# A fused two-block transformer kernel on one core: the gated unit in rounded halves, and the second head's first weights queued earlier

## What is computed

```python
# first block, per head h of 8 (weights of 128 columns each)
q, k, v, lx, ly = h_in @ w_in[...]              # five products 256x2048 by 2048x128
xc = causal_conv(lx); r, i = sigmoid(xc @ w_a), sigmoid(xc @ w_x)
a = exp(-8 r softplus(-lam)); state = scan(a, sqrt(1 - a*a) * i * xc)
attention(q, k, v); state * gelu(ly)
# second block, after the state-space scan
y = gelu(ssm(u)); y = y * sigmoid(y @ w_glu + b_glu)   # the gated unit, w_glu 2048x2048
out = (y * silu(z)) @ w_out
```

## Time and profile before

| | us |
|---|---|
| median of three runs (lowest, highest) | 3626.04 (3616.76, 3626.87) |
| profiled execution | 3616.24 |
| its span | 3614.5 |
| TensorE busy | 3435.4 (95% of the span) |
| VectorE busy | 2457.7 (68%) |
| ScalarE busy | 1337.0 (37%) |

### The profile page before, as it was taken

How to read it: one execution, slowest core, us unless ns; L and a number is a source line. 1 busy time by engine, 2 the same in 40 slices (tenths; PEclk the granted TensorE clock), 3 DMA queues, 4 the chain that set the end, 5 groups by cost and what they waited for, 6 DMA issues and landing times. The chain is left out here.

```text
span 3614.5 us, 56289 instructions
## 1 busy us (share of the span) xinstructions
PE 3435.4 (95%) x20628; PEld 3038.4 (84%) x20628; DVE 2457.7 (68%) x4574; ACT 1337.0 (37%) x1960; POOL 354.0 (10%) x400
## 2 busy tenths in 40 slices
PE   3899999999999999999999998999999899999998
PEld 2688887889777999999999997676679898999998
DVE  7666556867487777777777777888835634666665
ACT  1232311013244444444444444211112434555553
POOL 0010110000000000000000000677710000000000
PEclk8999999999999999999999999999999999999999
DMA  9678743446777888888888885222247644555543
GB/s 404 269 302 302 273 168 128 157 144 235 288 286 292 294 295 294 291 292 296 296 295 296 296 293 200 82 89 91 91 171 253 253 144 138 187 187 184 184 171 139
DMA packets 123316, 817.71 MB, mean 226 GB/s; under 512 B 12848, under 2 KB 18224, under 8 KB 27184
## 3 DMA queue, kind: packets, MB, share of 16 engines
q1 hardware_dynamic: 105696, 761.31, 58.4%
q10 hardware_dynamic: 17488, 54.58, 4.0%
HBM read 791.65 MB, written 24.18 MB: 226 GB/s over the span
## 5 line engine op out<-in xcount | busy, mean ns | idle before, releaser
L526 PE MATMUL bank<-H,ring 128*128 128x256 f32 x3680 | 828.8, 384 | 30.3 <-PEq L371 13.4
L526 PEld LDWEIGHTS bank<-H,ring 128*128 128x128 f32 x3680 | 696.9, 192 | 149.8 <-issue 51.3
L1833 DVE TENSOR_TENSOR vlo<-ring,vhi 128x1024 fp32r<-128x1024 f32 x448 | 547.4, 1225 | 289.1 <-ACT vhi L1241 287.8
L1241 ACT ACTIVATE vhi<-ring 128x1024 fp32r<-128x1024 f32 x448 | 474.0, 1060 | 606.9 <-PE bank L596 315.0
L562 PE MATMUL bank<-Hhi,whi 128*128 128x256 f32 x1920 | 484.9, 290 | 20.9 <-DVE Hlo L1530 9.6
L1519 DVE TENSOR_TENSOR wlo<-ring,whi 128x1024 fp32r<-128x1024 f32 x240 | 293.9, 1232 | 304.7 <-ACT whi L1054 301.4
L563 PE MATMUL bank<-Hlo,whi 128*128 128x256 f32 x1920 | 475.1, 285 | 0.0
L589 PE MATMUL bank<-vhi,Ghi 128*128 128x512 f32 x1024 | 402.0, 393 | 15.2 <-ACT vhi L1241 15.2
L590 PE MATMUL bank<-vhi,Glo 128*128 128x512 f32 x1024 | 401.1, 392 | 0.0
L562 PEld LDWEIGHTS bank<-Hhi,whi 128*128 128x128 f32 x1920 | 370.8, 193 | 31.0 <-issue 17.7
L541 PE MATMUL bank<-Fhi,vhi 128*128 128x256 f32 x1536 | 373.0, 279 | 1.1 <-ACT vhi L1241 1.1
(11 more groups left out here) (422 smaller groups left out, 4374.2 us busy)
## 6 DMA issues: line engine op xcount, KB each, us to landing
ring<-in_peer_u SPq DMA_DIRECT2D x128, 1024.0 KB, 5.7
ring<-in_peer_v SPq DMA_DIRECT2D x128, 1024.0 KB, 5.9
arena<-in_w_mod SPq DMA_DIRECT2D x96, 1024.0 KB, 7.1
ring<-in_w_ada SPq DMA_DIRECT2D x72, 1024.0 KB, 7.1
ring<-in_w_qz SPq DMA_DIRECT2D x64, 1024.0 KB, 4.8
ring<-in_w_in SPq DMA_DIRECT2D x35, 1024.0 KB, 7.3
ring<-in_ssm_in SPq DMA_DIRECT2D x32, 1024.0 KB, 5.0
ring<-in_w_mod SPq DMA_DIRECT2D x32, 1024.0 KB, 5.0
```

Source lines behind the costliest of these rows:

```text
L526: last = mm(out, ring[:, pos % R, k, :], rhs[:, k, :], start=(k == 0), stop=(k == KT - 1))
L1241: A(vhi[:, half], v_half(pos, half), ACT.Copy).then_inc(s("vhi_ready"), 1)
L1833: v.tensor_tensor(vlo[:, half], v_half(pos, half), vhi[:, half].bitcast(F32), ALU.subtract)\
```

## The change

Three edits:

1. The gated unit's 16 products go from `gemm` to `gemm_split`. ScalarE and VectorE now also make high and low parts of Y after the gelu (`Yhi`, `Ylo`, in the place of the experts' old buffers `Fhi`, `Flo`) and of each weight chunk. The converting of chunk g+1 stands ahead of the sigmoid of product g on ScalarE, and ahead of the gating of product g on VectorE. `half_done` now starts counting at this stage, so the offsets in `LATE` grow by 16.
2. SyncE's order around heads 0 and 1: the first weight chunk of head 1 goes ahead of the three `head_vec` chunks and of the vector chunk of position 7, the second one right behind that chunk; the wait for `f_in_psum` is gone (`head_free`, which TensorE raises at the same point, remains). Head 1 is written out instead of being the loop's first turn; its own order is the same.
3. VectorE does the vector chunk of position 5 of head 0 ahead of `vectors(0)` instead of behind it.

```diff
-        LATE = dict(ssm_out=0, kv=16, nsa=40, w_o=104)
+        LATE = dict(glu=0, ssm_out=16, kv=32, nsa=56, w_o=120)
 # SyncE
-            for pos in range(8):
-                if pos in FIRST:
-                    head_skip(pos)
-                else:
-                    head_load(0, pos)
-            sp.wait_ge(s("f_in_psum"), 1)
+            for pos in (0, 1):
+                head_skip(pos)
+            head_load(0, 2)
+            for pos in (3, 4):
+                head_skip(pos)
+            head_load(0, 5)
+            head_load(1, 0)
             for n in range(3):
                 head_beside(0, n)
-            with sp.Fori(1, HEADS) as i:
-                for pos in range(2):
-                    head_load(i, pos)
+            head_load(0, 7)
+            head_load(1, 1)
+            head_skip(6)
+            def rest_of_head(i):
                 sp.wait_ge(s("gates_in_psum"), i + 1)
                 sp.dma_start(gate_w, a["gate_w"][i]).then_inc(s("gatew_loaded"), 16)
                 for pos in range(2, 8):
                     head_load(i, pos)
                     if pos in (2, 4, 6):
                         head_beside(i, pos // 2 - 1)
+            rest_of_head(1)
+            with sp.Fori(2, HEADS) as i:
+                for pos in range(2):
+                    head_load(i, pos)
+                rest_of_head(i)
 # TensorE
-            pe.wait_ge(s("y_gelu"), 4)
+            pe.sem_inc(s("half_done"), 2)
             for g in range(16):
-                gemm("glu", 0, GLU_W[g], banks[g % 4][:, 0:T], g % 4, uses[g % 4] + g // 4, Y)
+                gemm_split("glu", 0, GLU_W[g], g, banks[g % 4][:, 0:T], g % 4, uses[g % 4] + g // 4,
+                           rows=0 if g == 0 else None, pair=(Yhi, Ylo), made="y_rows")
 # ScalarE
             for j in range(4):
-                A(Y[:, 4 * j:4 * j + 4, :], Y[:, 4 * j:4 * j + 4, :], ACT.Gelu_apprx_tanh).then_inc(s("y_gelu"), 1)
+                A(Y[:, 4 * j:4 * j + 4, :], Y[:, 4 * j:4 * j + 4, :], ACT.Gelu_apprx_tanh)
+                act.drain()
+                A(Yhi[:, 4 * j:4 * j + 4, :], Y[:, 4 * j:4 * j + 4, :], ACT.Copy).then_inc(s("yhi_ready"), 1)
+                if j == 1:
+                    high("glu", 0, GLU_W[0], 0)
             for g in range(16):
-                product(act, "glu", 0, GLU_W[g])
+                if g < 15:
+                    high("glu", 0, GLU_W[g + 1], g + 1)
+                late_product(act, "glu", g)
 # VectorE
+                whole_vec("heads", i, 5, 33 + 3 * i)
                 if first:
                     vectors(i)
-                whole_vec("heads", i, 5, 33 + 3 * i)
...
+            for j in range(4):
+                dve.wait_ge(s("yhi_ready"), j + 1)
+                v.tensor_tensor(Ylo[:, 4 * j:4 * j + 4, :], Y[:, 4 * j:4 * j + 4, :],
+                                Yhi[:, 4 * j:4 * j + 4, :].bitcast(F32), ALU.subtract).then_inc(s("y_rows"), 4)
+                if j == 1:
+                    low("glu", GLU_W[0], 0)
             for g in range(16):
+                if g < 15:
+                    low("glu", GLU_W[g + 1], g + 1)
                 dve.wait_ge(s("sig_ready"), g + 1)
```

More of the change, by code:

```diff
@@ L285, in build @@
         P1 = WD[:].rearrange("p (a b) -> p a b", a=2)
-        glt, P2 = r(2, T), r(2, T)
+        P2 = r(2, T)
+        rb = Region(2 * KT * T)
+        glt, gated = rb(2, T), rb(2, T)
+        Yhi, Ylo = Fhi, Flo
         Z = r(2, 2, T)
@@ L359, in build @@
                      "masks_built u_ready bu_in_psum bu_read frac_ready table_ready z_ready q_ready "
-                     "y_pair gelu_free glu_free y_read y_gelu sig_ready w1_loaded kv_ready vr_in_psum vr_ready "
+                     "y_pair gelu_free glu_free y_read yhi_ready y_rows sig_ready w1_loaded kv_ready vr_in_psum vr_ready "
                      "cmp_gelu cmp2_in_psum kc_ready vc_in_psum vc_ready gt_in_psum gates_copied gates_turned cmp_in_psum cmp_added mask_ready vg_ready q_ready2 "
@@ L549, in gemm_experts, with gemm_split @@
                     last.then_inc(s("v_used"), 1)
-            def gemm_split(stage, i, pos, c, out, bank, need=None, halves=(0, 1), rows=None):
+            def gemm_split(stage, i, pos, c, out, bank, need=None, halves=(0, 1), rows=None, pair=(Hhi, Hlo), made="h_ready"):
                 if need is not None:
@@ L560, in gemm_split @@
                         if rows is not None:
-                            pe.wait_ge(s("h_ready"), rows + kk + 1)
-                        mm(out, whi[:, half, k, :], Hhi[:, kk, :], start=(kk == 0), stop=False)
-                        mm(out, whi[:, half, k, :], Hlo[:, kk, :], start=False, stop=False)
+                            pe.wait_ge(s(made), rows + kk + 1)
+                        mm(out, whi[:, half, k, :], pair[0][:, kk, :], start=(kk == 0), stop=False)
+                        mm(out, whi[:, half, k, :], pair[1][:, kk, :], start=False, stop=False)
                     pe.wait_ge(s("wlo_ready"), n + 1)
@@ L566, in gemm_split @@
                         kk = 8 * half + k
-                        last = mm(out, wlo[:, half, k, :], Hhi[:, kk, :], start=False, stop=(kk == KT - 1))
+                        last = mm(out, wlo[:, half, k, :], pair[0][:, kk, :], start=False, stop=(kk == KT - 1))
                         if half == 1 and k == 0:
@@ L908, in _ @@
                 uses[b] += 8
-            pe.wait_ge(s("y_gelu"), 4)
+            pe.sem_inc(s("half_done"), 2)
             for g in range(16):
-                gemm("glu", 0, GLU_W[g], banks[g % 4][:, 0:T], g % 4, uses[g % 4] + g // 4, Y)
+                gemm_split("glu", 0, GLU_W[g], g, banks[g % 4][:, 0:T], g % 4, uses[g % 4] + g // 4,
+                           rows=0 if g == 0 else None, pair=(Yhi, Ylo), made="y_rows")
             for b in range(4):
                 uses[b] += 4
-            pe.sem_inc(s("half_done"), 2)
             for g in range(16):
@@ L2024, in gated_low @@
                     .then_inc(s("h_ready"), 1)
+            for j in range(4):
[4 more added lines that the diff above has]
+                    low("glu", GLU_W[0], 0)
             for g in range(16):
+                if g < 15:
+                    low("glu", GLU_W[g + 1], g + 1)
                 dve.wait_ge(s("sig_ready"), g + 1)
-                v.tensor_tensor(P2[:, g % 2, :], glt[:, g % 2, :], Y[:, g, :], ALU.mult)
+                v.tensor_tensor(gated[:, g % 2, :], glt[:, g % 2, :], Y[:, g, :], ALU.mult)
                 dve.drain().then_inc(s("glu_free"), 1)
-                v.tensor_tensor(SZ[:, g, :], P2[:, g % 2, :], SZ[:, g, :], ALU.mult).then_inc(s("sz_made"), 1)
+                v.tensor_tensor(SZ[:, g, :], gated[:, g % 2, :], SZ[:, g, :], ALU.mult).then_inc(s("sz_made"), 1)
                 if g > 0:
```

## The result

The changed kernel takes 3600.06 us (median of five runs, 3597.54 to 3601.38). The kernel before, run beside it, takes 3616.76 us (median of five, 3615.69 to 3626.87). The ratio is 0.9942, with a 95% interval from 0.9925 to 0.9959: faster by 0.6%. The profiled execution of the changed kernel took 3601.38 us, that of the kernel before 3616.24, a gain of 14.9 us.

A forecast was written before the change was run, and what follows sets the result against it. TensorE, busy 95% of the span, was taken as the bound. Gains of 11.2 us (gated unit) and 4.0 (heads) sum to 15.2, taken from the median 3626.04: forecast 3610.8 us, range 3597 to 3622.

The forecast's parts named there:

- Rate of a product: Gated unit: a product takes 5.76 us in rounded halves instead of 6.91, saving TensorE 1.15 us each.
- The new wait: Gated unit: TensorE waits 0.5 us for `whi` in each pair of products, seven times, 3.5 us in all.
- Start and end of the unit: Gated unit: first product ends 14.6 us after the gelu's start (0.8 lost); first `ssm_out` product takes 7.8 (1.3 lost).
- the case for which the prediction had 13.9: Gated unit's start: with TensorE at full clock all through, the first product ends 13.9 us after the gelu's start.
- Heads: Heads 0 and 1: stop ahead of head 1 goes, 3.0 us stop before its third product; gain 4.0 us (1.2 to 7.0).
- Nothing later: After the gated unit: nothing depends on more than the shift, as TensorE's stream sets the order again; no further change.
- The late slot: Rival, load behind `glu`'s vector chunk: landing in 9.0 us makes pairs 16.0 us, 12.8 us slower, 3638.8; chance 0.08.
- The stops did show: Answers the rival that waits in `glu` and before head 1's third product don't show: gain 21.7 us, 3604.3; chance 0.22.
- The clock rival: Clock falls in new pauses: 2.8 us lost at head 1, 2.4 at the unit's first product; gain 10.0, 3616.0; chance 0.20.
- 3601.0 in its terms: Whole kernel: the profiled execution's 3616.24 us less the forecast gain of 15.2 us.

The follow-up runs named there:

- edit 1 alone: Gated unit in rounded halves, heads left as in the kernel before, against the kernel before: 3605.15 us (eight runs), ratio 0.9968.
- edits 2 and 3 alone: Queue's new order and moved vector chunk of head 0, gated unit as before, against the kernel before: 3615.23 us (12 runs), ratio 0.9989.
- the edit of that stage: State-space stage's phase fraction formed without a VectorE SBUF-to-SBUF operation: 3596.67 us on the changed kernel, 3587.38 on that with vector chunks of gated unit and head 0 moved.
- the long execution with the even vector chunks: Changed kernel with `glu`'s vector chunk behind every even product instead of every odd one: 3600.58 us (six runs), ratio 0.9944; this profiled execution spans 3608.1 us.

## Why the prediction was right, and where it was wrong

- **Rate of a product.** 5.76 us forecast, 5.68 measured, so 1.2 us less over fifteen products. The row of `ssm_out` was a good measure for the same matmuls in another stage.
- **The new wait.** Where it was put and why held: ScalarE waits for `w_glu`, TensorE for `whi`, before even products from the fourth on, and moving the vector chunk removes it. The issue was forecast 5.9 us after the start of product g+1 and came 6.1 after it (2649.93 to 2656.01). Seven stops of 0.5 were 3.5 us; measured are 90.0 - 15 x 5.68 = 4.8 us, of which 3.1 are six waits that the profile names. The seventh place, ahead of `ssm_out`, shows 0.16 us. Fifteen products with the stops: 89.9 forecast, 90.0 measured. That this is so close is luck: the rate's part was 1.2 us too high and the stops' 1.3 too low, most of that through one late load.
- **Start and end of the unit.** 14.6 us forecast and 13.7 measured for the start: TensorE reached full clock sooner than half way (at 2640.63 in the rows a matmul takes 0.12 us, before it 0.21; the clock is 0.56 from 2635.9 to 2640.6 and 1.00 from there to 2644.3), so it waited for the last low parts of Y, and these set the end. That is the case for which the prediction had 13.9. For the first product of `ssm_out` 7.8 forecast, 2742.05 - 2734.28 = 7.8 measured, with the stop on `Hlo` in it. Sum: 112.3 forecast, 111.5 measured, so 12.0 us gained where 11.2 were forecast. In the profile of edit 1 alone it is 13.5.
- **Heads.** A stop of 3.0 us ahead of the third product, a start at 156.5 and a gain of 4.0; measured 2.86, 156.05 and 4.47. The load went out 0.45 us earlier than forecast and landed 5.0 us later as forecast. That edit 3 lets the second chunk land in time held, and in the one run without it the gain was nil.
- **Nothing later.** "Nothing later depends on more than this shift" did not hold for the profiled execution: 16.1 us of lead at the first product of `ssm_out` became 14.8 at the end, through a fall of the clock to 0.50 at a stop of 1.84 us. That 15.2 us forecast meet 14.9 measured is therefore in part luck.
- **Rivals.** The late slot cost 45 us where a variant forced it, and did not happen in the changed kernel. The stops did show. The clock rival happened in some executions: not behind the heads' stop of the changed kernel's profile (1.00), fully in that of edits 2 and 3 alone (0.50, and 3.0 us lost).
- **The step that failed** is the last of the sum: "Against the median of 3626.04 the forecast is 3610.8." The gain of 15.2 us was right (14.9 between the profiled executions, 16.7 between the medians), and so was "3601.0 in its terms", for a measured 3600.06. But the three runs then shown, 3616.76 and two near 3626.5, were not a spread about one value. By their times they were one run of a shorter group and two of a longer, and the median of three fell into the longer. Five runs gave 3616.76. Subtracting a gain read from a short execution (its span 3614.5) from a median of long ones put the forecast 10.7 us too high. Against the five-run median the same gain gives 3601.6. The text had the facts in hand: it put its profile with the lowest of the three runs and saw that "executions of one kernel lie 10 us apart", and still took the median for its base.

The longer group is no property of the change: the kernel before has it. In the two long executions that were profiled (both of variants, none of the kernel before) 11.2 and 11.5 us of it lie in a stage that no edit touches. How often it comes is open. The changed kernel had none of it in five runs, edit 1 alone two in eight, and whether that is chance these counts can't say. That the group goes with the edit of that stage is shown by twelve runs out of twelve; why it goes, and that nothing else contributes, is not.

## What to carry to other kernels

When the runs of a kernel fall in two groups, forecast from the profiled execution's own time and say which group it is in; a median of three is a toss between them. A move in a queue is worth what the next slot allows: ask for each load behind it who frees its slot, since without the second edit here the first only pushed the stop one product on. Where a vector operation from SBUF to SBUF runs beside GpSimd, look at its single lengths (here 0.35 to 1.40 us) and not at the mean, and try it with an operand or result in PSUM if the place is there.

## What was not expected of the hardware

**Two engines seem to fall into a rhythm that holds itself.** With this stage unchanged, one VectorE operation (128x256, fp32, from SBUF to SBUF) takes 539 to 546 ns on average in six profiled executions and 1014 to 1019 in two, for the whole stage; GpSimd's wait for VectorE's queue beside it grows from 35.6 to 83.7 us, and the stage is 11 us longer. VectorE's operation is long where it starts behind GpSimd's, since it ended 0.15 us after that one in all 47 cases counted above; and what GpSimd then waits for is VectorE's queue (0.67 us ahead of 2519.64 in the rows above), so that they start together again (0.11 us apart there). That this loop is what holds the state is read from these rows and not shown by itself. The opening said that the engines meet only through semaphores. That does not cover these rows: in the changed kernel's trace one and the same operation of VectorE takes 0.35 or up to 1.40 us with GpSimd's operation beside it, and the kernel has no semaphore between its start and its end.

What holds VectorE's operation up is not shown. The rows show this much: from SBUF to SBUF it takes 0.35 us where it starts first and up to 1.4 where GpSimd's runs already, and the same operation into PSUM takes 0.47 to 0.48 us each time in all eight profiles (473 to 484 ns in the changed kernel's, where 46 of the 64 start while an operation of GpSimd is running). Runs of one and the same kernel lie in both groups (7 of 19 and 7 of 11 of the kernel before in the longer), so which state it is seems to be settled anew in each execution.

**A stop of nearly the same length may or may not lower TensorE's clock.** 2.86 us did not in one profile (1.00 behind it), 2.82 us did in another (0.50), at a price of 3.0 us; 1.84 us did in the changed kernel's `ssm_out` (0.50, 1.4 us) and did not at the same place before (1.00). In the long execution with the even vector chunks 2.68 us cost 1.7 (0.50 from 156.7 to 160):

```profile
156.68 8.82 PE L538 MATMUL bank<-H,ring 128*128 128x256 f32 x32 [2.68 <-DMA ring<-in_w_in]
```

against 7.17 and 10.15 us for the same product. From these profiles I estimate such a stop, in a forecast for this kernel, at its length and a chance of 1.4 to 3 us more; and two executions can differ by several such falls with no edit between them, as in the experts above (four against two).
